# Two blocks of a transformer in one kernel: where the weight splits of the feed-forward stages stand in each engine's order

## The reference, cut to what matters

```python
mod_l = jax.nn.silu(c) @ ada_w[l] + ada_b[l]
...
xl = post_norm(xl, 0.5 * g1 * swiglu(modulate(xl, sh1, sc1), ffn1_w_in[l], ffn1_w_out[l]))
...
def swiglu(h, w_in, w_out):
    gate, up = jnp.split(h @ w_in, 2, axis=-1)
    return (jax.nn.silu(gate) * up) @ w_out
def post_norm(x, y):
    return layer_norm(ALPHA * x + y)
```

## Time and profile before

| what | before |
|---|---|
| time, median of 3 executions | 2168.76 us (2166.93 to 2169.74) |
| the profiled execution's own time | 2166.41 us |
| its span in the trace | 2164.6 us |
| mean granted TensorE clock in it | 0.978 of full speed |
| TensorE busy | 2070.7 us, 96% |
| DVE busy | 1360.0 us, 63% |
| ACT busy | 754.0 us, 35% |

### The profile page before, as it was taken

The page is one execution under the profiler, slowest core; times in us unless marked ns, Lnnn a source line. Parts: engine busy times, 40 slices in busy tenths (PEclk is TensorE's granted clock), DMA queues, the critical chain, the costliest instruction groups (busy, mean ns, idle before and its releaser), DMA issues. The chain is left out here.

```text
span 2164.6 us, 28984 instructions
## 1 busy us (share of the span) xinstructions
PE 2070.7 (96%) x12096; PEld 1769.0 (82%) x12096; DVE 1360.0 (63%) x2086; ACT 754.0 (35%) x941; POOL 149.8 (7%) x129
## 2 busy tenths in 40 slices
PE   7999999999999899999999999899999989998997
PEld 7979978878887787777878887788888879678997
DVE  5955965776774557646876774555555455565555
ACT  4464465221222434435221222522122242554332
POOL 0500500000002000030000002000000200020001
PEclk9999999999999899999999999899999999998999
DMA  6743644554543210222554543333442333123552
GB/s 230 237 148 127 236 158 152 187 190 165 192 157 118 91 42 6 103 97 83 188 188 166 193 154 118 117 134 110 165 146 86 118 147 137 40 79 130 174 175 87
DMA packets 69227, 301.32 MB, mean 139 GB/s; under 512 B 6128, under 2 KB 24176, under 8 KB 49136
## 3 DMA queue, kind: packets, MB, share of 16 engines
q1 hardware_dynamic: 66384, 290.06, 38.6%
q10 hardware_dynamic: 2720, 9.51, 1.2%
HBM read 298.50 MB, written 1.05 MB: 138 GB/s over the span
## 5 line engine op out<-in xcount | busy, mean ns | idle before, releaser
L383 PE MATMUL PS<-xh,wh 128*128 128x512 f32 (+1 forms) x3772 | 1034.0, 349 | 9.6 <-DVE wh L344 4.8
L383 PEld LDWEIGHTS PS<-xh,wh 128*128 128x128 f32 x3772 | 680.8, 189 | 103.2 <-DVE wh L344 5.1
L383 PE MATMUL PS<-xl,wh 128*128 128x512 f32 (+1 forms) x2134 | 727.4, 341 | 0.0
L340 ACT ACTIVATE wh<-raw 128x2048 fp32r<-128x2048 f32 (+3 forms) x226 | 386.8, 1712 | 313.7 <-PE PS L383 230.0
L344 DVE TENSOR_TENSOR wh<-raw,wh 128x2048 fp32r<-128x2048 f32 (+3 forms) x188 | 388.1, 2065 | 141.4 <-ACT wh L340 141.0
L383 PEld LDWEIGHTS PS<-xl,wh 128*128 128x128 f32 x2134 | 405.4, 190 | 44.6
L383 PE MATMUL PS<-HH,wh 128*128 128x512 f32 (+1 forms) x1408 | 397.4, 367 | 6.9 <-DVE wh L344 6.7
L383 PEld LDWEIGHTS PS<-HH,wh 128*128 128x128 f32 x1408 | 252.8, 188 | 56.6 <-DVE wh L344 9.2
L842 DVE CUSTOM_DVE_ANT_0 NRM<-SQ,CBR 128x1024 f32<-128x1024 f32 x240 | 284.0, 1221 | 6.1 <-DVE mod L842 0.5
L383 PE MATMUL PS<-HL,wh 128*128 128x512 f32 (+1 forms) x704 | 258.0, 366 | 0.0
L786 ACT ACTIVATE SI<-PS 128x512 f32<-128x512 f32 (+1 forms) x88 | 48.1, 547 | 602.3 <-PE PS L383 577.6
(11 more groups left out here) (358 smaller groups left out, 1943.2 us busy)
## 6 DMA issues: line engine op xcount, KB each, us to landing
raw<-ffi_dram SPq DMA_DIRECT2D x88, 1024.0 KB, 5.0
SQ<-adat_dram SPq DMA_DIRECT2D x120, 512.0 KB, 3.7
raw<-ffo_dram SPq DMA_DIRECT2D x64, 704.0 KB, 4.2
raw<-layer_dram SPq DMA_DIRECT2D x36, 1024.0 KB, 5.0
lent<-layer_dram SPq DMA_DIRECT2D x14, 1024.0 KB, 7.5
raw<-odd_dram SPq DMA_DIRECT2D x12, 1024.0 KB, 4.8
raw<-even_dram SPq DMA_DIRECT2D x9, 1024.0 KB, 4.9
raw<-eout_dram SPq DMA_DIRECT2D x4, 1024.0 KB, 4.8
```

The lines of the kernel that those rows point to most:

```text
L340: act.activation(high(i)[:, 0:n], raw[:, i.slot, 0:n], ACT.Copy).then_inc(hi_done, 1)
L383: m = pe.matmul(out, w[rows, o:o + P], x, start=n == 0 and j == 0, stop=n == len(tiles) - 1 and j == 2)
```

## The change

Four things are done.

- In every feed-forward half, DVE splits the rest of the second output slab in the step of the last input slab, ahead of that step's modulation sums. It did this in the first output slab's step, behind them.
- In stage 0 the slab pair is no longer mixed: TensorE works through the first slab whole and then through the second.
- In stage 5 the third slab is split by halves: ACT writes the high part of columns 0 to 1023, then of 1024 to 2047; DVE the rest of each half as it comes; TensorE starts on the gate chunk when the first half is there, and waits again before the up chunk.
- In stage 5 X is multiplied by ALPHA in two halves of 1024 columns, one in the third slab's step, one in the fourth's.

```diff
@@ -344,6 +344,36 @@
             eng.tensor_tensor(low(i)[:, 0:n], raw[:, i.slot, 0:n], high(i)[:, 0:n].bitcast(F32),
                               ALU.subtract).then_inc(lo_done[who], 1)
 
+        HALVED = FIRSTS[5:]
+
+        def halved_hi(act, i):
+
+            act.wait_ge(slab_full[i.slot], 16 * (i.turn + 1))
+            act.wait_ge(slab_used, i.base - 1)
+            half = SIZE[i.base] // 2
+            act.activation(high(i)[:, 0:half], raw[:, i.slot, 0:half], ACT.Copy).then_inc(on["halved_hi"], 1)
+            act.activation(high(i)[:, half:2 * half], raw[:, i.slot, half:2 * half], ACT.Copy).then_inc(hi_done, 1)
+
+        def halved_lo(dve, i):
+
+            half = SIZE[i.base] // 2
+            dve.wait_ge(on["halved_hi"], 1)
+            dve.tensor_tensor(low(i)[:, 0:half], raw[:, i.slot, 0:half], high(i)[:, 0:half].bitcast(F32), ALU.subtract)\
+                .then_inc(on["halved_lo"], 1)
+            dve.wait_ge(hi_done, HI[i.base] + 1)
+            dve.tensor_tensor(low(i)[:, half:2 * half], raw[:, i.slot, half:2 * half], high(i)[:, half:2 * half].bitcast(F32),
+                              ALU.subtract).then_inc(lo_done["dve"], 1)
+
+        def dense_halved(pe, i, n):
+
+            pe.wait_ge(on["halved_lo"], 1)
+            pe.wait_ge(drained[i.par], i.d // 2)
+            for c in range(2):
+                if c:
+                    wait_split(pe, i)
+                m = product(pe, PS[:, 2 * i.par + c, 0:n], i, [((c * KT + k) * P, xh[:, k, 0:n], xl[:, k, 0:n]) for k in range(KT)])
+            m.then_inc(slab_used, 1)
+
         def k_half(slab_, n):
 
             return slab_.rearrange("p (c k q) -> p c k q", c=2, k=KT)[:, :, n * KT // 2:(n + 1) * KT // 2, :]
@@ -404,8 +434,12 @@
 
 
             slab_begin(pe, i)
-            order = [(0, 0), (0, 1), (0, 2), (1, 0), (0, 3), (1, 1), (0, 4), (1, 2), (0, 5), (0, 6), (1, 3), (0, 7)]
-            for s, k in order + [(1, k) for k in range(4, KT)]:
+            if i.base == FIRSTS[0]:
+                order = [(s, k) for s in range(2) for k in range(KT)]
+            else:
+                order = [(0, 0), (0, 1), (0, 2), (1, 0), (0, 3), (1, 1), (0, 4), (1, 2), (0, 5), (0, 6), (1, 3), (0, 7)]
+                order += [(1, k) for k in range(4, KT)]
+            for s, k in order:
                 j = i + s
                 if (s, k) == (1, 0):
                     slab_begin(pe, j)
@@ -624,10 +658,13 @@
                         mm = act.activation(xh[:, k, cols], X[:, k, cols], ACT.Identity, bias=shift(k), scale=scale(k))
                 mm.then_inc(on["xm_hi"], 1)
 
-        def act_scale(act, m):
+        def act_scale(act, m, parts=(slice(0, KT),)):
 
             act.wait_ge(on["xm_lo"], KT * (m + 1))
-            act.activation(X[:, :, 0:WIDTH[m]], X[:, :, 0:WIDTH[m]], ACT.Copy, scale=ALPHA).then_inc(on["x_scaled"], 1)
+            for part in parts:
+                mm = act.activation(X[:, part, 0:WIDTH[m]], X[:, part, 0:WIDTH[m]], ACT.Copy, scale=ALPHA)
+            if part.stop == KT:
+                mm.then_inc(on["x_scaled"], 1)
 
         def dve_modulate(dve, m, norm, centre=None):
 
@@ -784,9 +821,15 @@
                         act_ahead(act, i)
                     act.wait_ge(slab_used, i.count(4, i.base + 1))
                     act.activation(SI[:, i.par, 0:n], PS[:, 2 * i.par, 0:n], ACT.Silu).then_inc(on["gate_act"], 1)
-                    if i.base in FIRSTS:
+                    if i.base in HALVED:
+                        halved_hi(act, i + 2)
+                    elif i.base in FIRSTS:
                         act_ahead(act, i)
-                    if i.base - 2 in FIRSTS:
+                    if i.base - 2 in HALVED:
+                        act_scale(act, m, (slice(0, KT // 2),))
+                    elif i.base - 3 in HALVED:
+                        act_scale(act, m, (slice(KT // 2, KT),))
+                    elif i.base - 2 in FIRSTS:
                         if m == 2:
                             conditions(act, 1)
                         act_scale(act, m)
@@ -807,7 +850,10 @@
             l, f, j, n = FFN_STAGES[m]
             dense_pair(pe, Idx(FIRSTS[m]), n if m else T, KT * m)
             for k in range(2, FH):
-                dense(pe, Idx(FIRSTS[m] + k), 2, KT, xh, xl, 0, n)
+                if FIRSTS[m] in HALVED and k == 2:
+                    dense_halved(pe, Idx(FIRSTS[m] + k), n)
+                else:
+                    dense(pe, Idx(FIRSTS[m] + k), 2, KT, xh, xl, 0, n)
             for half in range(2):
                 if half:
                     runs_of(pe, f"ffi{f}{l}1", lambda i, k: dense(pe, i, 2, KT, xh, xl, 0, n))
@@ -864,13 +910,18 @@
                     dve.tensor_copy(hh, hf).then_inc(on["h_hi"], 1)
                     dve.wait_ge(on["h_hi"], k + (h0 + 1))
                     dve.tensor_tensor(hl, hf, hh.bitcast(F32), ALU.subtract).then_inc(on["h_lo"], 1)
-                    if i.base in FIRSTS:
+                    if i.base in HALVED:
+                        halved_lo(dve, i + 2)
+                    elif i.base in FIRSTS:
                         dve_ahead(dve, i)
+                    if k == FH - 1:
+                        dve_ahead(dve, i + 1)
                     chunk_sums(dve, i)
                 steps_of(f"ffi{f}{l}{half}", hidden)
 
                 def down(i, k):
-                    dve_ahead(dve, i)
+                    if k:
+                        dve_ahead(dve, i)
                     if half == 0 and k == 0:
                         dve.wait_ge(on["x_scaled"], m + 1)
                     dve.wait_ge(slab_used, i.count(4, i.base + 1))
```

More of the change, by code:

```diff
@@ L506, in segments @@
             return SM3[u % 3][:, 0:SEGS[UNITS[u]] * w].rearrange("p (g k) -> p g k", k=w)[:, :, 0:n]
-        names = """xl_written mix_rest x_chunk v_done cz_zero tr_ready mod_cols late_in ctx_in kc_raw conv_done
+        names = """halved_hi halved_lo xl_written mix_rest x_chunk v_done cz_zero tr_ready mod_cols late_in ctx_in kc_raw conv_done
                     sq_ready sq_folded one_set rstd_ready rms_rows first_hi first_lo half_lo rms_in rms_out xm_written perms_done roped blk_ready idx_scores_out idx_relu idx_used scores_out
```

## The result

| | before | after |
|---|---|---|
| time, median | 2168.64 us (2166.93 to 2169.74, 4 executions) | 2152.06 us (2149.16 to 2155.52, 4 executions) |
| ratio to before, 95% interval | | 0.9925 [0.9912, 0.9937] |
| the profiled execution | 2166.41 us, span 2164.6 | 2155.52 us, span 2153.7 |
| mean granted TensorE clock in it | 0.978 | 0.977 |

The change gained 16.6 us, 4 more than the 12.6 predicted, and its median lies 0.4 us under the low end of the range. In all, twelve executions of the changed kernel were timed, with a median of 2149.5 us (2148.56 to 2155.52); the one behind the first profile is the slowest of them.

What follows compares the result with a forecast made beforehand. TensorE, busy 2070.7 of 2164.6 us, was taken as the bound. Gains of 2.2 (stage 0's slab pair), 7.8 (early second-slab split) and 2.6 us (stage 5 halves) sum to 12.6: 2168.8 becomes 2156.2 us, range 2152.5 to 2161.5.

Steps and rivals of the forecast that it cites:

- the seven stops: TensorE's waits for DVE's weight splits in stages 0, 2 and 5; removing them was to gain 12.6 us.
- the pair: Stage 0's first two slabs, worked whole by whole: the wait before the next slab goes entirely, gaining 2.2 us.
- half 0: First feed-forward half of stages 0 and 2: wait before the second output slab goes, 1.53 us in each stage.
- half 1: Second feed-forward half of stages 0 and 2: wait before the second output slab goes, 2.37 us in each stage.
- third slab: In stage 5, split by halves: TensorE starts once the first half is ready, gaining 1.7 us.
- fifth slab: In stage 5, multiplying by ALPHA in halves delays the high part less; the wait goes, gaining 0.9 us.
- rivals 1 and 2: Waits return one slab later, 2161.1 us, chance 6%; idle time only moves, no measurable change, 2164.5 to 2169, chance 5%.
- The halved instructions: The 1024-column instructions in stage 5: 1.06 us each on ACT, 1.22 us each on DVE.
- third output slab in half 0: In stages 0 and 2, its split was to be ready with 1.6 us to spare, so no new wait.
- the one stretch of the earlier trace with a 2.1 us stop: Stage 0, 642 to 660 us: granted clock read as 1.00, taken as evidence against a clock-caused slowdown.
- rival 3: At the starts of stages, more time at TensorE's low clock makes the kernel slower, for instance 2176 us; chance 3%.

## Why the prediction was wrong by 4 us

**Right: the seven stops.** 12.6 us were predicted, 12.3 measured (predicted in brackets): the pair 2.2 (2.2), half 0 1.43 each (1.53), half 1 2.3 (2.37), third slab 1.8 (1.7), fifth slab 0.85 (0.9). None came back later: rivals 1 and 2 did not happen. The halved instructions cost what the rows said, ACT 1.05 and DVE 1.22 us each. One of the prediction's times is added up wrongly, without harm: 467.08 + 8.0 gives 475.1 us, not 474.8, for the third output slab in half 0, so 1.9 us were to spare there.

**Wrong: the step that left the clock out of the sum.** The prediction took 1.00 in the one stretch of the earlier trace rows with a 2.1 us stop as if it held in every execution, and let the clock in only as rival 3, for the worse. So the clock's term behind the stops was put at nothing. It pays the other way: with the stops go the falls of the clock behind them. Averages over four traces of before and five of after differ by 16.6 us in span:

| term | us |
|---|---|
| the stops' own length | 12.3 |
| low clock behind the pair's stop (2 of 4 traces, 1.6 each) | 0.8 |
| low clock behind stage 2's last stop (2 of 4, 1.5 each) | 0.8 |
| low clock behind the third slab's stop in stage 5 (2 of 4, 1.5 each) | 0.7 |
| ahead of stage 0, where no instruction differs | 0.6 |
| the rest, at the starts of stages 2, 3 and 5 and at the end | 1.4 |

So 2.3 of the 4.3 us above the stops' length are low clock seen right behind the stops, and 0.6 are chance, as the place shows. The rest has 0.8 us before stage 3 and 0.6 before stage 5, where traces of one and the same kernel differ by 2 us and more; that it comes from the change is not shown. Nor is it shown where the two further us lie by which the medians of all executions (2149.5 against about 2168) differ more than these traces. The runs were also made on several chips: the three new traces of before come from another chip than the three new ones of the change, and on the chip of the latter the kernel before took 2162.82 us in its one execution, 13 us more than they. What of the difference is the chip's stays open.

Over all traces with at least one of the seven stops left open, a low stretch begins behind 12 of 59 of them, and unevenly: 3 of 7 at the pair, 1 of 9 at stage 0's half 1, 4 of 9 at stage 2's, 4 of 8 at the third slab of stage 5, and none of 26 at the three shorter ones (0.65 to 1.26 us idle). The Trainium skill (page "TensorE: Matmul & The Clock Gate", section "HAM oscillation — how this bites in real kernels") puts the cost of such a fall at the slow time less what full speed would have taken, half of it. The traces agree: behind the stop at 1301 us 8 matmuls start in three us instead of 15, and a fall costs 1.5 to 1.6 us. The Trainium skill (the same page, section "What's actually happening") also says that the chip looks at TensorE's activity at moments of its own, not tied to the kernel's start. The traces agree: the same kernel had three falls or none.

**Wrong: the range.** Its low end took the three executions' spread, 2.8 us; later the kernel before spread from 2162.7 to 2172.3 and once to 2175.6. The measured median lay only 0.4 us below that end, and the first four executions of the change were slow ones for it: over all twelve the median is 2149.5.

## What to carry to other kernels

A short stop of TensorE inside dense work can cost more than its length, since the granted clock may fall behind it in part of the executions: look at the clock behind each stop in several traces, and add an expected value for it to the gain of removing the stop. Holding the clock up with idle matmuls where TensorE waits for another engine made this kernel 9 us slower. Read small terms between fixed instructions of several traces, because whole-kernel medians that wander by several us hide them; and before a shorter stretch is credited to a change, look at the stretch ahead of it, which may be longer by as much.

## What was not expected of the hardware

Between two stages it mattered to within 3 us when the granted clock fell: in the changed kernel the way from stage 2's last addition to stage 3's first `xl` took 11.05 us in the trace where the clock fell 1.8 us behind the addition, and 8.9 to 9.2 us in the four where it fell after 4.0 to 4.7. And the part ahead of stage 0's first `HF` took between 354.8 and 357.3 us in the four traces of before, and between 353.4 and 358.4 in the ten traces of kernels that do not differ up to there: 5 us of chance before the change's first instruction.
